# Four moves within the head stage of a decoder kernel: low-rank part, attention copies, convolution taps, start of the inverse

## What is computed

```python
for l in range(2):
    x = layer_norm(ALPHA * x + 0.5 * swiglu(x, ffn1[l]))
    f_r, f_s, f_g = split(x @ w_in[l])
    x = layer_norm(ALPHA * x + concat(rwkv7(f_r), window_attention(f_s), gated_delta(f_g)) @ w_out[l])
    x = layer_norm(ALPHA * x + 0.5 * swiglu(x, ffn2[l]))
# rwkv7, 4 heads of 64: decay from tanh(wd) @ w_up, rate from ad @ a_up, gate sigmoid(gd) @ g_up;
#   a state recurrence over the tokens, group norm, gate
# gated_delta, 4 heads of 64: silu of a causal convolution with 4 taps, l2 norms;
#   a chunked recurrence, each chunk with a triangular solve; rms norm, gate
```

## Time and profile before

| | us |
|---|---|
| runs of the kernel (3), median | 3004.49 |
| lowest and highest of them | 2995.5, 3006.26 |
| the profiled execution, its own time | 3005.59 |
| its span, first to last instruction | 3003.8 |
| TensorE busy in the span | 2742.8 |
| VectorE busy | 1669.7 |
| ScalarE busy | 949.2 |
| mean granted TensorE clock | 0.901 |

### The profile page before, as it was taken

How to read it: one execution, slowest core, us unless ns; L and a number is a source line. 1 busy time by engine, 2 the same in 40 slices (tenths; PEclk the granted TensorE clock), 3 DMA queues, 4 the chain that set the end, 5 groups by cost and what they waited for, 6 DMA issues and landing times.

```text
span 3003.8 us, 59208 instructions
## 1 busy us (share of the span) xinstructions
PE 2742.8 (91%) x23222; PEld 2561.6 (85%) x23222; DVE 1669.7 (56%) x2503; ACT 949.2 (32%) x1694; POOL 161.5 (5%) x168
## 2 busy tenths in 40 slices
PE   8999999978796989999999999998887778999997
PEld 8999998866675889999999999987765668999996
DVE  5666347745545466664366653566445553666534
ACT  4333233322212243332233332344212222433323
POOL 1030110000000010001100001000000000100011
PEclk9999999976766999999999999998766768999998
DMA  4852234100000323232223222431000012222221
GB/s 110 101 93 86 85 107 121 44 27 1 9 9 1 91 66 90 85 89 83 86 78 88 87 85 85 129 90 41 7 1 8 9 28 86 77 84 84 87 87 59
DMA packets 380501, 201.67 MB, mean 67 GB/s; under 512 B 41461, under 2 KB 376821, under 8 KB 379528
## 3 DMA queue, kind: packets, MB, share of 16 engines
q1 hardware_dynamic: 377928, 197.46, 22.8%
q0 software_dynamic: 2400, 1.82, 1.9%
HBM read 188.07 MB, written 13.34 MB: 67 GB/s over the span
## 4 chain that ended last, share of the span: by engine, by line
PE 78%; DVE 10%; issue 5%; ACT 4%; DMA 1%; SPq 1%; DVEq 0%; POOLq 0%; ACTq 0%; POOL 0%
PE ps L682 51%; PE ps L737 25%; DVE ar L1918 3%; DVE ar L1912 2%; ACT ar L1415 2%; DVE wl L1796 1%; ACT wh L1346 1%; SPq L529 1%; PE ps L1011 1%; DVE x L1912 1%; DMA raws<-in_ffn_w_in 0%; DVE xl L1903 0%; DVE ar L1948 0%; ACT xh L1415 0%; DMA raws<-in_w_in 0%
## 5 line engine op out<-in xcount | busy, mean ns | idle before, releaser
L1796 DVE TENSOR_TENSOR wl<-raws,wh 128x1024 fp32r<-128x1024 f32 x336 | 411.3, 1225 | 673.1 <-ACT wh L1346 668.7
L737 PE MATMUL ps<-ar 64*64 64x64 f32 (+13 forms) x5408 | 517.6, 292 | 146.3 <-ACT ar L1415 39.0
L682 PE MATMUL ps<-xh,wh 128*128 128x272 f32 x2880 | 604.8, 291 | 17.7 <-DVE wl L1796 15.2
L737 PEld LDWEIGHTS ps<-ar 64*64 64x64 f32 (+6 forms) x5408 | 388.7, 177 | 250.2 <-issue 71.8
L682 PE MATMUL ps<-xh,wl 128*128 128x272 f32 x2880 | 599.7, 290 | 0.0
L682 PE MATMUL ps<-xl,wh 128*128 128x272 f32 x2880 | 598.3, 289 | 0.0
L1346 ACT ACTIVATE wh<-raws 128x1024 fp32r<-128x1024 f32 x336 | 354.7, 1057 | 416.6 <-PE ps L682 376.6
L682 PEld LDWEIGHTS ps<-xh,wh 128*128 128x128 f32 x2880 | 457.6, 190 | 21.4 <-DVE wl L1796 17.9
L682 PEld LDWEIGHTS ps<-xl,wh 128*128 128x128 f32 x2880 | 457.8, 190 | 0.0
L682 PEld LDWEIGHTS ps<-xh,wl 128*128 128x128 f32 x2880 | 457.3, 190 | 0.0
L682 PE MATMUL ps<-hh,wh 128*128 128x272 f32 x1408 | 292.3, 289 | 0.0
(11 more groups left out here) (188 smaller groups left out, 2749.9 us busy)
## 6 DMA issues: line engine op xcount, KB each, us to landing
raws<-in_ffn_w_in SPq DMA_DIRECT2D x176, 512.0 KB, 3.7
raws<-in_ffn_w_out SPq DMA_DIRECT2D x64, 512.0 KB, 4.0
raws<-in_w_in SPq DMA_DIRECT2D x42, 512.0 KB, 3.7
raws<-in_ffn_w_out SPq DMA_DIRECT2D x32, 384.0 KB, 3.4
raws<-in_w_out SPq DMA_DIRECT2D x16, 448.0 KB, 4.0
x_kept<-x SPq DMA_DIRECT2D x2, 2176.0 KB, 10.1
x<-x_kept SPq DMA_DIRECT2D x2, 2176.0 KB, 7.9
ar<-in_consts SPq DMA_DIRECT2D x2, 1337.5 KB, 6.7
```

The costliest lines, as they stand in the source:

```text
L682: ins = pe.matmul(ps[:, bank + h, 0:n1 - h * NH], w[u % 2][:, k, :], a[:, k0 + k, h * NH:n1], start=(first and k == 0 and n == 0), stop=(l ...
L737: return pe.matmul(dst, lhsT, rhs, start=start, stop=stop, **kw)
L1796: dve.tensor_tensor(wl[u % 2][:, :, :], raw[u % 2][:, :, :], wh[u % 2][:, :, :].bitcast(F32), ALU.subtract).then_inc(sem("wl_done"), 1)
```

## The change

- ScalarE's two tanh of the low-rank rows move into the projection loop, after chunk g = PC - 2 = 20. VectorE's gate part no longer has xl ahead of it.
- The high and low copies of the prompt's attention output (xh by ScalarE, xl by VectorE) move into the first step of samples_attend. y_attn gets another place, over rows 0 to 3 of pair 0's U; the wait for attn_l goes from the first step of prepare(0) to ScalarE's exponentials of cum.
- In prepare_gdn the taps 0, 1 and 2 are in the first step, tap 3 in the second.
- After mask m = 7 VectorE writes the masked halves to BB_ (not VB) and ticks start. TensorE writes the identity to bank 2 with one product of 512 columns, once mask 6 is done, and adds the 16 products to it. The samples' V_s comes after masks 8 and 9 (start_s), then VB = BB_ + identity, and the memset.

```diff
@@ -234,7 +234,7 @@
                   + [("corner", 0), ("corner", 1), ("side", 0), ("side", 1)])
-INV_V = in_order([("start",)]
+INV_V = in_order([("start",), ("start_s",), ("begun",)]
                  + [e for li in range(1, len(LEVELS)) for e in
...
@@ -244,7 +244,7 @@
                   "conv_s": 6, "conv_t": 6, "cu": 16, "cu_copied": 16, "cum": 6, "cx": 14, "cx_copied": 16,
-                  "cy": 16, "cy_copied": 16, "d_seq": 196, "dec": 6, "dif": 4, "dif_e": 6, "dif_min": 6, "exps": 9,
+                  "cy": 16, "cy_copied": 16, "d_seq": 192, "dec": 6, "dif": 4, "dif_e": 6, "dif_min": 6, "exps": 9,
                   "g_mm": 2, "gate_e": 4, "gate_g": 2, "gate_in": 4, "gates_t": 1, "gd_state": 2, "ge": 2,
...
@@ -371,12 +371,12 @@
         M_NORM = M_WORK + 6 * NT
-        ck, _o = region(M_TMP, DEC_BATCH * P)
+        ck, _ = region(M_TMP, DEC_BATCH * P)
+        y_attn, _o = region(M_TMP, 4 * NT)
         kd, _o = region(_o, 2 * NT)
...
         stat, _o = region(_o, 40)
-        y_attn, _o = region(_o, 4 * NT)
         assert _o <= M_NORM
...
@@ -1048,10 +1048,15 @@
 
+                    pe.wait_ge(sem("gram_masked"), at(lay, "gram_masked", 10 * q + 7))
+                    pe.sem_inc(passed, 1)
+                    ones = cst("id64").rearrange("p (o n) -> p o n", o=1).broadcast_to([P, 8, HD])
+                    mm(ps[:, 2, :].rearrange("p (m n) -> p m n", m=8), ident, ones, stop=False, skip_group_check=True)
                     v_done("start")
...
                         for pr in halves64:
-                            mm(ps[pr, 2, m * HD:(m + 1) * HD], VB[pr, m, :], ident[pr, pr])
+                            mm(ps[pr, 2, m * HD:(m + 1) * HD], BB_[pr, m, :], ident[pr, pr], start=False, skip_group_check=True)
+                    v_done("start_s")
                     for hp in range(2):
...
@@ -1476,17 +1481,17 @@
                         take(action, s)
-
-                act.wait_ge(sem("y_copied"), at(lay, "y_copied", HALVES))
-                go(xh[:, 2:6, 0:SEQ], y_attn[:, :, 0:SEQ]).then_inc(*tick("attn_h"))
-                act.wait_ge(sem("shifted"), at(lay, "shifted", 7))
-                go(proj[0:32, 6, :], proj[0:32, 6, :], ACT.Tanh).then_inc(*tick("lora_t"))
-                go(proj[64:128, 6, :], proj[64:128, 6, :], ACT.Tanh, scale=0.5).then_inc(*tick("lora_t"))
+                    if g == PC - 2:
+                        act.wait_ge(sem("shifted"), at(lay, "shifted", 7))
+                        go(proj[0:32, 6, :], proj[0:32, 6, :], ACT.Tanh).then_inc(*tick("lora_t"))
+                        go(proj[64:128, 6, :], proj[64:128, 6, :], ACT.Tanh, scale=0.5).then_inc(*tick("lora_t"))
 
...
                     go(xe[:, :, :, 3:7], proj[:, GCH:GCH + 6, SEQ:NT].rearrange("p c (b t) -> p c b t", b=DEC_BATCH)).then_inc(*tick("xe"))
+                    act.wait_ge(sem("y_copied"), at(lay, "y_copied", HALVES))
+                    go(xh[:, 2:6, 0:SEQ], y_attn[:, :, 0:SEQ]).then_inc(*tick("attn_h"))
                     act.wait_ge(sem("tail_t"), at(lay, "tail_t", 3))
...
@@ -1537,7 +1542,8 @@
                     act.wait_ge(sem("ys"), at(lay, "ys", 1))
-                    act.wait_ge(sem("attn_l"), at(lay, "attn_l", 1 if q == 0 else 2))
+                    if q:
+                        act.wait_ge(sem("attn_l"), at(lay, "attn_l", 2))
                     if q == 1:
...
@@ -1552,6 +1558,7 @@
                     act.wait_ge(sem("cum"), at(lay, "cum", q + 1))
+                    act.wait_ge(sem("attn_l"), at(lay, "attn_l", 1))
                     go(U[:, 0:3, 0:SEQ].rearrange("p k (i n) -> p k i n", i=TILES),
...
@@ -2032,8 +2039,6 @@
 
-                dve.wait_ge(sem("attn_h"), at(lay, "attn_h", 1))
-                tt(xl[:, 2:6, 0:SEQ], y_attn[:, :, 0:SEQ], xh[:, 2:6, 0:SEQ].bitcast(F32), ALU.subtract).then_inc(*tick("attn_l"))
                 ts(par("a0h"), par("a0"), 0.5, None, ALU.mult, None).then_inc(*tick("ys"))
...
@@ -2046,6 +2051,8 @@
                                         proj[64 * (h % 2):64 * (h % 2) + 64, SCH + h // 2, SEQ:NT].rearrange("p (b t) -> p b t", b=DEC_BATCH)).then_inc(*tick("qm"))
+                    dve.wait_ge(sem("attn_h"), at(lay, "attn_h", 1))
+                    tt(xl[:, 2:6, 0:SEQ], y_attn[:, :, 0:SEQ], xh[:, 2:6, 0:SEQ].bitcast(F32), ALU.subtract).then_inc(*tick("attn_l"))
                     yield
...
@@ -2123,7 +2130,8 @@
                     dve.wait_ge(sem("attn_out"), at(lay, "attn_out", 32))
-                    dve.wait_ge(sem("attn_l"), at(lay, "attn_l", 1 if q == 0 else 2))
+                    if q:
+                        dve.wait_ge(sem("attn_l"), at(lay, "attn_l", 2))
                     if q == 1:
...
@@ -2196,21 +2204,18 @@
                     dve.wait_ge(sem("xe"), at(lay, "xe", 1))
-                    tap(0)
-                    yield
-                    dve.wait_ge(sem("d_seq"), last(lay, "d_seq"))
-                    tap(1)
+                    for k in range(3):
+                        tap(k)
+                        dve.wait_ge(sem("d_seq"), last(lay, "d_seq"))
+                    yield
+                    tap(3)
                     dve.wait_ge(sem("dif"), at(lay, "dif", 2 * c + 1))
...
                     yield
-                    dve.wait_ge(sem("d_seq"), last(lay, "d_seq"))
-                    tap(2)
                     dve.wait_ge(sem("dif"), at(lay, "dif", 2 * c + 2))
...
                     yield
-                    dve.wait_ge(sem("d_seq"), last(lay, "d_seq"))
-                    tap(3)
                     for n in range(3):
...
@@ -2258,28 +2263,34 @@
                             tt(dst, src, cst("gmask") if m < 8 else cst("gmask_s", NSAMP), ALU.mult).then_inc(*tick("gram_masked"))
+                        if m == 7:
+                            dve.wait_ge(sem("gram_masked"), last(lay, "gram_masked"))
+                            um = cst("umask1")
+                            for pr in halves64:
+                                tt(BB_[pr, :, :], gram[pr, :, P + pr.start:P + pr.stop], wide(um[pr], 8, HD), ALU.mult).then_inc(*tick("inv_v" if pr.start else "d_seq"))
                         if m % 2:
                             yield
+
+                wide = lambda ap, n, w: bc(ap.rearrange("p (o n) -> p o n", o=1), [ap.shape[0], n, w])
 
...
                     nl = len(LEVELS) - 1
-                    wide = lambda ap, n, w: bc(ap.rearrange("p (o n) -> p o n", o=1), [ap.shape[0], n, w])
                     um, lm = cst("umask1"), cst("lmask")
...
 
+                    dve.wait_ge(sem("gram_masked"), last(lay, "gram_masked"))
+                    tt(V_s, gram_s[:, :, NSAMP:2 * NSAMP], wide(ums, 2, NSAMP), ALU.mult).then_inc(*tick("d_seq"))
+                    dve.wait_ge(sem("d_seq"), last(lay, "d_seq"))
+                    tt(V_s, V_s, wide(ident[0:NSAMP, 0:NSAMP], 2, NSAMP), ALU.add).then_inc(*tick("inv_v"))
+                    dve.wait_ge(sem("inv_v"), at(lay, "inv_v", q * N_INV_V + 1))
+                    tt(VB, BB_, wide(cst("id64"), 8, HD), ALU.add).then_inc(*tick("inv_v"))
                     if q < 2:
                         dve.memset(V[HD:P, :, 0:HD], 0.0).then_inc(*tick("d_seq"))
-                    dve.wait_ge(sem("gram_masked"), last(lay, "gram_masked"))
-                    for pr in halves64:
-                        tt(VB[pr, :, :], gram[pr, :, P + pr.start:P + pr.stop], wide(um[pr], 8, HD), ALU.mult).then_inc(*tick("d_seq"))
-                    tt(V_s, gram_s[:, :, NSAMP:2 * NSAMP], wide(ums, 2, NSAMP), ALU.mult).then_inc(*tick("d_seq"))
-                    dve.wait_ge(sem("d_seq"), last(lay, "d_seq"))
-                    tt(V_s, V_s, wide(ident[0:NSAMP, 0:NSAMP], 2, NSAMP), ALU.add)
-                    tt(VB, VB, wide(cst("id64"), 8, HD), ALU.add).then_inc(*tick("inv_v"))
+                    dve.wait_ge(sem("inv_v"), at(lay, "inv_v", q * N_INV_V + 3))
                     yield
...
```

## The result

| | us |
|---|---|
| before, median of 4 runs beside it | 3005.38 |
| after, median of 4 runs (2919.62 to 2930.37) | 2922.48 |
| ratio, 95% interval | 0.9734, 0.9704 to 0.9764 |
| the profiled execution of after, its span | 2918.8 |
| TensorE busy, before and after | 2742.8, 2690.9 |

A forecast was written before the change was run, and what follows sets the result against it. No engine is full; what ends each TensorE idle stretch in the two head stages counts. Terms 1.1 + 4.7 + 2.1 + 6.3 = 14.2 us a layer, 28.4 for both, gave 2977.2, or median 2976; range 2958 to 2990.

The forecast's parts named there:

- the four places: TensorE's idle before first low-rank products, in two later pairs' first recurrence steps, and before inverse turns; 14.2 us a layer.
- rival 1: Head stages: fuller TensorE holds its clock, mean 0.68 to 0.70, 9 us a layer more, 2958 us; chance 0.15.
- Low-rank part: Before the first low-rank products: TensorE starts 4.8 us earlier, decay sums give back 3.7; 1.1 us a layer.
- the term's low end (-0.5): Decay sums: TensorE falls to the low clock waiting at the third tile; half of 3.15 us takes twice the time.
- Taps: Two later head pairs' first recurrence steps: taps moved into VectorE's idle gain 4.7 and 2.1 us a layer.
- Inverse: Turns opening the four inverses: less idle gains 1.6, 3.2, 0.4 and 1.1 us, sum 6.3 a layer.
- the stated other end: Pair 3's inverse turn at full clock: gain 2.9 us with the faster turn, instead of 1.1.
- They fall into VectorE's wait: After the inverse's start: VectorE's identity, samples' masks and memset fit its wait for the first product.
- The argument against rival 1: Pair 3's turn comes at half clock behind busy work, so small products alone don't lift the clock.
- The price of rival 1: Head stages: 308 busy us x 0.02/0.70 = 9 us a layer, giving 2958 us.

The follow-up runs named there:

- all eight stages: Kernel after with 0, 7, 13 or 20 extra products ahead of each head stage, two layers each: 2922.5, 2949.0, 2939.6, 2938.3 us.
- four starts: 0, 7, 13 or 20 extra products in the last projection chunk, added to kernels before and after: means 2999.8 and 2937.4 us.

## Why the prediction was wrong

**Which step failed.** "What pulls further is the clock of all the work behind the four places, which no term holds": the sum held the mean clock of a stage at 0.68, and that is where it broke. The step was named, priced by itself as rival 1 (0.70, 2958), and given 0.15. The rival's direction was right and its size was wrong: the clock rose to 0.77 at this start, and TensorE's busy time, left at 308 in the sum, measured 283. The terms of the four places were good in all. Their sum was 14.2 us a layer, and TensorE's idle fell by 15.5; both stages are about 352 us long and not 378.

**Part by part.**
- *Low-rank part.* Idle ahead of the first products 2.52 us (2.7 forecast); xl between the qm copies and the Newton step; TensorE held 4.28 us inside the sums (some 4). The exponentials start 20.54 us behind the last scaling, 20.71 before, so 0.2 is left and not 1.1. Six of the ten sums came behind the wait and not half, and they took 3.52 us at the low clock, the condition of the term's low end (-0.5); the first products, 3.93 us and not 4.74, gave some of it back. ScalarE's wait for the sample outputs fell from 8.66 us to 5.06 and held nobody.
- *Taps.* From tap 0 to the state copy 20.27 us became 15.47 in the third pair: 4.8 (4.7 forecast). In the fourth 16.12 became 13.87: 2.25 (2.1). TensorE's 5.51 us is 0.57. Its 7.32 is 2.02, but part of it has only moved ahead: in front of it now stands a wait of 2.45 us, where 0.43 stood before, so that together 4.5 us are still lost there (about 5 forecast).

```profile
800.27 0.69 PE L737 MATMUL ps<-ar 64*128 64x64 f32 x4 [0.57 <-DVE ar L1922]
...
893.47 0.48 PE L737 MATMUL ps<-ar 128*64 128x64 f32 x4 [2.45 <-DVE ar L2342]
...
896.41 0.69 PE L737 MATMUL ps<-ar 64*128 64x64 f32 x4 [2.02 <-DVE ar L2348]
```

- *Inverse.* Pair 1: 3.83 to 0.49 us, the turn in 1.15, as forecast. Pair 2: no idle. Pair 3: the forecast took the value at the low clock, 1.1 and a product of 2.05; the clock was full, product and turn 1.14 and 1.15, the stated other end. Pair 0: the samples' transposes start 51.9 us behind the last scaling (53.2 before), 1.3 earlier where 2.7 had been summed. TensorE is early there (turn 48.8) and then waits 1.81 us for VectorE, on which the identity's addition and the memset, 1.3 us, stand ahead of the normalising. "They fall into VectorE's wait" was wrong for this pair.
- *The argument against rival 1.* "Pair 3's turn comes at half clock behind busy work, so small products alone don't lift it" took a level of the kernel before for a property of the place. After the change the same turn takes 1.15 us in all eight stages.
- *The price of rival 1.* It took 0.02 in the clock. Its formula with the 0.09 that came, 308 x 0.09/0.77, gives 36 us a layer; the busy time fell by 24.6, or 29 without the identity products. The clock of a row is a mean over its idle time too (0.61 in a stretch with nothing busy), so the formula is rough; what part of the busy time follows the clock was not measured.

**What the runs put in its place.** At this start the two stages lost 31 us of idle and 49 of busy time. On the mean over four starts the gain is 62, some 36 of idle and 27 of busy time at a higher clock. The other 20 are, as far as four starts tell, luck: a poor start for the kernel before (391.3 us a stage, the mean is 386.2) and a good one for the kernel after (349.9, the mean is 354.6). Luck doesn't save the forecast: by the mean the result would be some 2942, still under the range. That the clock rises as the waits shrink is shown by these means and by the four stages without the identity product; which wait decides which fall was not settled, and the size of the product's share neither. The Trainium skill's page "TensorE: Matmul & The Clock Gate" (HAM oscillation) has the direction, that gaps between bursts throttle the clock. The traces agree with that: idle 85.6 us a stage and a clock of 0.68 to 0.72 before, 67.6 and 0.74 to 0.78 after.

## What to carry to other kernels

Where TensorE's clock has a mean well under 1.00 over a dependent stage, removed idle can count for more than itself: here a change that took 18 us of idle out of a layer made the stage 31.6 us shorter, some 1.8 times that, on the mean of four starts. Price that as part of the forecast, not as a rival, and set the range by how much such a stage moves when its start is moved by a microsecond or two. And test a change to such a stage at several starts before a few tenths of a percent are believed; a handful of repeated products ahead of it is enough.

## What the runs showed of the hardware

- Products whose result is thrown away can make a kernel faster: seven of 272 columns ahead of each stage, 13 us (ratio 0.9946, 0.9928 to 0.9964).
- The same code in the same stage takes 85.4 to 92.8 us (turn 0 to turn 1) from one start, and even one layer of an execution, to another, at 11 to 12 us of idle in each. The median of repeated runs at one start doesn't show this.
- Small differences go with a level: with no identity product and 0.43 us of idle ahead of the turn, the 132 products behind it took 2.9 to 3.0 us more in three stages of four. In the fourth they took no more, so the wait alone doesn't decide it.
